# Separate key and value loads, a key store in rows of its own, and chunk-wise merging for mixer C in a two-layer hybrid encoder

## The chip, the core and the metric

One core of a Trainium2 chip runs the whole kernel. The metric is the device time of one execution in microseconds (us). The core has a matrix engine (TensorE, PE in the profile), a vector engine (VectorE, DVE), a scalar engine (ScalarE, ACT), GpSimd (POOL) and a sync engine (SyncE, SP), which here issues every DMA. Each engine works through its own list of instructions in order and waits on semaphores that the others raise. Sixteen DMA engines move the data between the chip's memory (HBM) and the on-chip memory (SBUF); matrix results land in eight banks of PSUM.

## What is computed

Two layers over two sequences of 256 and 512 tokens, width 2048. In each layer one projection gives queries, keys, values and gates for three attention mixers, whose outputs are gated, joined and projected back:

```
h = rms_norm(x, ln_g[l])
qa, ka, va, ga, qb, kb, vb, gb, qc, kc, vc, gc = split(h @ w_in[l])
ya = window_sink_attention(...)      # A: +-128 tokens, learned sink, relative bias
yb = global_axial_attention(...)     # B: dense, rotary positions
yc = dilated_mixture_attention(...)  # C: (window, dilation) = (128,1), (512,4), (2048,16)
mix = concat[ya * silu(ga), yb * silu(gb), yc * silu(gc)]
x = x + mix @ w_out[l]
```

In mixer C each of the three groups g gives an output and the logarithm of its softmax denominator, and the outputs are summed with softmax weights over these logarithms (the merge). There are 12, 12 and 8 query heads of 64 columns for A, B and C, and a quarter as many key and value heads.

## The kernel before, in words

The 768 tokens are six tiles of 128. A layer runs in three parts: the input projection (nine slabs of 512 columns, each 16 chunks deep), the attention with the gate projection woven in, and the output projection (four slabs). Every product is made of three matmuls on halves called hi and lo; weights arrive as `w_raw` and are split by ACT (`w_hi`) and DVE (`w_lo`).

At the end of the projection of a slab each head block is normalised, transposed and split, and SP stores it with four DMAs a tile into the DRAM tensor `heads_t` (tile, partition, block, 128 tokens), queries and keys alike; values go to `v_rows`. The values of the last slab go out in `store_values(l, NS_IN - 1, t)`, six DMAs.

The attention is a list of 216 steps a layer, in four sections. Section Q: four units of six steps, the dilated groups of mixer C, four heads a step (the "quads"). Section A: three units, 72 steps. Section C: the undilated group, two units, 48 steps. Section B: three units, 72 steps. In sections A, B and C an item is one tile for a pair of heads and takes two steps. A unit has one key head and one value head. All engines run the same loop over turns i: PE does `scores(i)`, some pieces of the gate projection (2.4 a turn in A, B and C, 0.6 in Q), then `p_turn(i - 3)` and the product with the values, `pv(i - 4)` or `pair_pv(i - 5)`. DVE does `find_minima(i)`, ACT `exp_step(i)`. `scores(i)` may not run until `find_minima(i - 2)` has freed its bank. The first `find_minima` of a layer waits until all value stores have landed (`v_stored`), since its output lies over the buffer that they read.

Loads. `load_unit(l, u)` brings keys and values of a unit into one of two slots: four DMAs for the keys (64 partitions each, six runs of 512 B in each partition) and one for the values, all counted on `kv_loaded`; it waits until the product with the values of the unit two before is done, and SP reaches it two items before the new unit begins. `load_item(l, it)` brings the queries of an item, four slots, and waits for the scores of the item four before. `load_bias` brings a unit's bias rows, four DMAs for a quad unit. All of them, the weights and the stores lie in SP's one list, in the order written in the loop over `it`. Before the loop the order is `load_bias(0)`, `load_unit(0)`, four `load_item`, six `store_values`, `load_unit(1)`, `load_bias(1)`.

The merge. Quads leave their outputs and statistics in DRAM (`part_rows`). In section C each item loads them back (`part_in`, three slots), DVE works out weights in ten short instructions (`merge_minima`, `merge_weights`) with ACT's exponential in between, POOL scales and adds the parts (`merge`), and `finish_item` on DVE adds the item's own output, which lies in `o_bank[0]`. The next item's product writes that same bank, so `pv` waits for it:

```
                if st["r"] != 1 and it >= 1:
                    old = ITEMS[it - 1]
                    if old["kind"] == "Q":
                        pe.wait_ge(part_taken, l * N_QUADS + old["quad_no"] + 1)
                    elif old["kind"] == "C":
                        pe.wait_ge(mixed, l * N_PAIRS + old["pair_no"] + 1)
```

PE then transposes the finished item (`mix_turn`) into bank 5 and ACT copies it out (`mix_copy`).

Of the kernel before, what the change touches and what calls it, by code (L numbers as in the profile page):

```python
# [35 lines left out]
P = 128  # L36
# [58 lines left out]
def index_units():  # L95

    blocks = vs = 0
    at = {}
    for u in itertools.chain(*SLAB_UNITS):
        if UNITS[u][0] == "v":  # L100
            at[u] = vs
            vs += 1
        else:
            at[u] = blocks
            blocks += 1
    return at, blocks, vs


PLACE, BLOCKS, VHEADS = index_units()
# [54 lines left out]
SLAB_BLOCKS = [sum(r[3] for r in HEAD_RUNS[s]) for s in range(NS_IN)]  # L164
MAX_BLOCKS = max(SLAB_BLOCKS)

# [96 lines left out]
N_TURNED = N_PAIRS - N_MERGES  # L263
SUNK = np.cumsum([x["kind"] == "A" for x in STEPS]).tolist()
# [20 lines left out]
PART_IN_SLOTS = 3  # L285
STAT_SLOTS = 8
# [5 lines left out]
MIN_LAG = 1  # L292
MERGE_LAG = 1
WEIGHT_LAG = 2
# [3 lines left out]
X_LAG = 7  # L298
NORM_LAG = 1
PAIR_LAG = 5  # L300
FOLD_LAG = 6

# [90 lines left out]

def piece_schedule():
# [48 lines left out]
PRODUCT_TURN = [max(SILU_TURN[n], CHUNK_LAST[n] + X_LAG) + 1 for n in range(GATE_TILES)]  # L443
# [18 lines left out]
UNITS_AT = at_items((u, UNIT_LAST[u - KV_SLOTS] + V_LAG + 1) for u in range(KV_SLOTS, len(ATT_UNITS)))  # L462
# [5 lines left out]
def build(nc, x_prompt, x_sample, ln_g, w_in, q_norm_a, k_norm_a, sink_a, q_norm_b, k_norm_b,  # L468
          q_norm_c, k_norm_c, rel_bias, w_out, selector, rope, identity, y_prompt, y_sample):
    with ExitStack() as ctx:  # L470
# [7 lines left out]
        heads_t = dram("heads_t", [TT, P, BLOCKS * P])  # L478
        v_rows = dram("v_rows", [TOKENS, VHEADS * DH])
# [47 lines left out]
        mix = sb("mix", [P, 2, P])  # L527
        part_sum = sb("part_sum", [P, 2, 2, P])
        merge_min = sb("merge_min", [P, PART_IN_SLOTS, 2])
        merge_w = sb("merge_w", [P, PART_IN_SLOTS, 3, 2])  # L530
        merge_d = sb("merge_d", [P, PART_IN_SLOTS, 3, 2])
# [25 lines left out]
        part_in = sb("part_in", [P, PART_IN_SLOTS, 2, PART])  # L557
# [6 lines left out]
        v_split = sb("v_split", [P, TT, 2 * DH], F32R)  # L564
        prob = sb("prob", [P, P_SLOTS, P_COLS])
# [5 lines left out]
        quad_t = sb("quad_t", [P, Q_SLOTS, 4, P], F32R)  # L571
        top[0] = pt_at
# [26 lines left out]
        mix_bank = bank[5]  # L599
# [55 lines left out]
        kv_loaded = [sem(f"kv_loaded{i}") for i in range(KV_SLOTS)]  # L655
        bias_loaded = [sem(f"bias_loaded{i}") for i in range(2)]
        part_loaded = [sem(f"part_loaded{i}") for i in range(PART_IN_SLOTS)]
# [14 lines left out]
        merge_parts = sem("merge_parts")  # L672
        recips = sem("recips")
# [35 lines left out]
        def mixed_chunk(item):  # L709

            return CHUNK_ORDER.index(item["unit"]["chunk"] + item["hp"])

# [88 lines left out]

        def turned_parts(l, s, t):
# [15 lines left out]
        def turned_views(eng, l, i, parts):  # L818
# [5 lines left out]
            eng.wait_ge(pv_done, l * N_STEPS + free)  # L824
            src = pt_bank[(l * N_STEPS + i) % PT_BANKS][:, 0:st["tiles"] * P].rearrange("p (j n) -> p j n", n=P)
            return src, parts[:, a % 2, 0:st["tiles"], st["r"], :]

        def heads_in_dram(eng, l):

            for i in range(2):  # L830
                eng.wait_ge(heads_stored[i], 16 * 4 * ((heads_before(l + 1) + 1 - i) // 2))
# [5 lines left out]
        def _(sp):  # L837
# [26 lines left out]
            def stores(l, slot):  # L864
                for step, s, t in POST.get(slot, ()):
                    if step == "sums" and V_RUNS[s]:
                        store_values(l, s, t)
                    if step == "store" and HEAD_RUNS[s]:
                        i = HEAD_AT[l, s, t]
                        sp.wait_ge(turned_lo, i + 1)  # L870
                        b0, nb = PLACE[SLAB_UNITS[s][HEAD_RUNS[s][0][2]]], SLAB_BLOCKS[s]
                        for part in range(2):
                            dst = heads_t[t, part * DH:(part + 1) * DH, b0 * P:(b0 + nb) * P].rearrange("p (b e c) -> p b e c", e=2, c=P)
                            for e in range(2):
                                sp.dma_start(dst[:, :, e, :], turned[e * DH:(e + 1) * DH, i % 2, part, 0:nb // 2, :].bitcast(F32))\
                                    .then_inc(heads_stored[i % 2], 16)

            def load_unit(l, u):
# [8 lines left out]

                for part in range(2):
                    src = heads_t[:, part * DH:(part + 1) * DH, unit["k"] * P:(unit["k"] + 1) * P].rearrange("t p n -> p t n")
                    for to in range(2):  # L890
                        sp.dma_start(k_t[to * DH:(to + 1) * DH, slot, :, part, :].bitcast(F32), src)\
                            .then_inc(kv_loaded[slot], 16)
                if unit["kind"] == "Q":
                    sp.wait_ge(v_stored, 16 * (l * V_STORES + V_BEFORE_LAST))
                sp.dma_start(v_t[:, slot, :, :],
                             v_rows[:, unit["v"] * DH:(unit["v"] + 1) * DH].rearrange("(t p) n -> p t n", p=P))\
                    .then_inc(kv_loaded[slot], 16)
# [20 lines left out]
            def load_item(l, it):  # L918
# [11 lines left out]
                if item["kind"] == "C":  # L930
                    m = l * N_MERGES + item["merge_no"]
                    if m % N_MERGES == 0:
                        for i in range(PART_SLOTS):
                            sp.wait_ge(part_stored[i], 16 * (l + 1) * (N_QUADS // PART_SLOTS))
                    if m >= PART_IN_SLOTS:

                        sp.wait_ge(merge_parts, 2 * (m - PART_IN_SLOTS + 1))
                    sp.dma_start(part_in[:, m % PART_IN_SLOTS, :, :],
                                 part_rows[t * P:(t + 1) * P, :, unit["j"], hp, :]).then_inc(part_loaded[m % PART_IN_SLOTS], 16)
# [53 lines left out]
            for l in range(DEPTH):  # L993
# [28 lines left out]
                load_unit(l, 0)  # L1022
                for it in range(Q_SLOTS):
                    load_item(l, it)
                for t in range(TT):
                    store_values(l, NS_IN - 1, t)
                load_unit(l, 1)
                load_bias(l, 1)
                for it in range(Q_SLOTS, N_ITEMS + 1):
                    if it < N_ITEMS:  # L1030
                        load_item(l, it)
                    for u in UNITS_AT.get(it, ()):
                        if ATT_UNITS[u]["kind"] != "Q":
                            sp.wait_ge(v_stored, 16 * V_STORES * (l + 1))
                        load_unit(l, u)
                    for b in BIASES_AT.get(it, ()):
                        load_bias(l, b)
                    for i in PARTS_AT.get(it, ()):
# [33 lines left out]
        def _(pe):  # L1072
# [45 lines left out]
            def project_chunk(l, c):  # L1118
# [8 lines left out]
                for t in range(TT):  # L1127
                    if k == 0:
# [10 lines left out]
                        elif s == NS_IN and t == 4:  # L1139
                            pe.wait_ge(mixed, (l + 1) * N_PAIRS)  # L1140
# [34 lines left out]
            def scores(l, i):  # L1175
# [3 lines left out]
                if st["r"] != 1:  # L1179
                    pe.wait_ge(q_loaded[it % Q_SLOTS], 16 * (it // Q_SLOTS + 1))  # L1180
                    if st["t"] == 0 and st["hp"] != 1:
                        kv, times = kv_place(l, st["u"])
                        pe.wait_ge(kv_loaded[kv], 16 * 5 * times)
# [30 lines left out]
            def pv(l, i):  # L1214
# [4 lines left out]
                if st["r"] != 1 and it >= 1:  # L1219

                    old = ITEMS[it - 1]
                    if old["kind"] == "Q":
                        pe.wait_ge(part_taken, l * N_QUADS + old["quad_no"] + 1)
                    elif old["kind"] == "C":
                        pe.wait_ge(mixed, l * N_PAIRS + old["pair_no"] + 1)
                    else:
                        pe.wait_ge(mixed, l * N_PAIRS + old["pair_no"])
                values = v_t[:, kv_place(l, st["u"])[0], :, :]
# [802 lines left out]
```

## Time and profile before

| | |
|---|---|
| median of 3 runs | 3000.72 us (2998.91 to 3005.28) |
| the profiled execution | 2995.85 us, its span 2994.1 us |
| PE busy | 2907.6 us (97%) |
| DVE, ACT, POOL busy | 46%, 38%, 31% |
| mean granted TensorE clock | 0.983 |
| DMA, one queue, 340 MB | 39.5% of sixteen engines |

The profile gives for each engine its instructions, grouped by the line of the kernel; the idle time of the engine just before them and what ended it; the clock that the chip granted TensorE in a stretch, as a share of its full speed; and the issue and landing of each DMA. A wait that is put down to "issue" is one for which the profile shows no releaser. Matmuls are pipelined, so that a busy PE isn't a PE at its peak.

### The profile page before, as it was taken

Reading aid. Unit: us, or ns where it says so; the run is one execution under the profiler, and the core shown is the slowest. Engines: PE = TensorE matmul, PEld = TensorE weight load, DVE = VectorE, ACT = ScalarE, POOL = GpSimd, SP = SyncE. Lnnn points to the kernel's source line nnn. Section 1 sums busy time; section 2 is a strip of 40 time slices with the busy share of each in tenths; the row PEclk is TensorE's granted clock in tenths of the full one; section 3 lists DMA queues with packets and bytes.
Section 4 is the critical chain, followed back from the end, with each engine's and each line's share of the span. In section 5 each row is a group of like instructions: output and inputs, shape, how many; then the busy total and the mean of one; then the engine's idle time right before and its main releaser. Section 6 shows DMA issues by size and latency. Waiting matters only on the chain. (4 is left out here: it accounts for less than half of the span.)

```text
span 2994.1 us, 44065 instructions
## 1 busy us (share of the span) xinstructions
PE 2907.6 (97%) x15201; PEld 2580.0 (86%) x15201; DVE 1376.2 (46%) x3869; ACT 1143.6 (38%) x2865; POOL 942.8 (31%) x942
## 2 busy tenths in 40 slices
PE   8999999998998999999999999999989989999999
PEld 6888899988998899888888888998889988998887
DVE  3334433324777777522323344333247777775221
ACT  4322232225664466421322322222346644664110
POOL 0333323310664477300002333323007634772000
PEclk9999999998999999999999999999879999999999
DMA  4333334357443432433223433334664434324332
GB/s 163 84 111 103 108 105 113 108 153 187 116 118 90 127 105 75 148 122 106 99 85 90 110 111 104 99 99 111 174 166 116 121 90 130 102 71 155 110 101 92
DMA packets 409305, 342.80 MB, mean 114 GB/s; under 512 B 53527, under 2 KB 340407, under 8 KB 409084
## 3 DMA queue, kind: packets, MB, share of 16 engines
q1 hardware_dynamic: 409084, 339.98, 39.5%
q8 instruction: 123, 2.02, 0.3%
q14 instruction: 98, 0.80, 0.1%
HBM read 256.03 MB, written 83.86 MB: 114 GB/s over the span
## 5 line engine op out<-in xcount | busy, mean ns | idle before, releaser
L1144 PE MATMUL bank<-w_hi,act_hi 128*128 128x512 f32 x2496 | 1000.5, 401 | 4.3 <-DVE w_lo L1561 4.3
L1145 PE MATMUL bank<-w_lo,act_hi 128*128 128x512 f32 x2496 | 988.8, 396 | 0.0
L1146 PE MATMUL bank<-w_hi,act_lo 128*128 128x512 f32 x2496 | 988.7, 396 | 0.0
L1561 DVE TENSOR_TENSOR w_lo<-w_raw,w_hi 128x512 fp32r<-128x512 f32 x544 | 388.5, 716 | 640.7 <-ACT w_hi L1323 638.8
L1323 ACT CAST w_hi<-w_raw 128x512 fp32r<-128x512 f32 x544 | 335.8, 618 | 778.7 <-PE bank L1146 775.7
L1144 PEld LDWEIGHTS bank<-w_hi,act_hi 128*128 128x128 f32 x2496 | 517.8, 207 | 95.2 <-DVE w_lo L1561 5.2
L1146 PEld LDWEIGHTS bank<-w_hi,act_lo 128*128 128x128 f32 x2496 | 517.7, 207 | 94.7
L1145 PEld LDWEIGHTS bank<-w_lo,act_hi 128*128 128x128 f32 x2496 | 518.1, 208 | 88.9
L1924 POOL TENSOR_SCALAR prob<-prob,denom 128x256 f32<-128x256 f32 (+2 forms) x288 | 343.4, 1198 | 323.6 <-DVE denom L1694 323.4
L1167 PE MATMUL bank<-act_hi,w_hi 128*128 128x384 f32 x1024 | 351.2, 343 | 0.0
L1169 PE MATMUL bank<-act_hi,w_lo 128*128 128x384 f32 x1024 | 348.3, 340 | 0.0
L1168 PE MATMUL bank<-act_lo,w_hi 128*128 128x384 f32 x1024 | 347.8, 340 | 0.0
L1915 POOL TENSOR_TENSOR y<-y,gains 128x256 f32<-128x256 f32 (+1 forms) x144 | 153.0, 1076 | 317.5 <-DVE y L1594 317.5
L1627 DVE TENSOR_TENSOR turned<-bank,turned 128x512 fp32r<-128x512 f32 (+1 forms) x96 | 63.2, 658 | 340.4 <-ACT turned L1386 340.4
L1210 PE MATMUL bank<-ident,prob 128*128 128x128 f32 x1232 | 213.9, 281 | 5.3 <-POOL prob L1924 5.3
L1685 DVE TENSOR_TENSOR pt_lo<-bank,pt_hi 128x256 fp32r<-128x256 f32 (+2 forms) x288 | 153.5, 533 | 125.6 <-ACT pt_hi L1418 122.6
L1418 ACT CAST pt_hi<-bank 128x256 fp32r<-128x256 f32 (+2 forms) x288 | 132.9, 461 | 186.6 <-PE bank L1210 176.6
L1168 PEld LDWEIGHTS bank<-act_lo,w_hi 128*128 128x128 f32 x1024 | 195.9, 191 | 4.2
L1167 PEld LDWEIGHTS bank<-act_hi,w_hi 128*128 128x128 f32 x1024 | 195.5, 191 | 4.2
L1386 ACT CAST turned<-bank 128x512 fp32r<-128x512 f32 (+1 forms) x96 | 53.8, 560 | 375.9 <-PE bank L1115 375.9
L1169 PEld LDWEIGHTS bank<-act_hi,w_lo 128*128 128x128 f32 x1024 | 195.7, 191 | 0.0
L1210 PEld LDWEIGHTS bank<-ident,prob 128*128 128x128 f32 x1232 | 161.2, 145 | 16.9 <-POOL prob L1924 6.9
(97 smaller groups left out, 3579.9 us busy)
## 6 DMA issues: line engine op xcount, KB each, us to landing
w_raw<-w_in SPq DMA_DIRECT2D x144, 512.0 KB, 4.1
heads_t<-turned SPq DMA_DIRECT2D x336, 128.0 KB, 2.4
w_raw<-w_out SPq DMA_DIRECT2D x64, 512.0 KB, 4.1
q_t<-heads_t SPq DMA_DIRECT2D x192, 128.0 KB, 2.1
k_t<-heads_t SPq DMA_DIRECT2D x96, 192.0 KB, 3.6
w_raw<-w_in SPq DMA_DIRECT2D x32, 448.0 KB, 3.5
quad_t<-heads_t SPq DMA_DIRECT2D x48, 256.0 KB, 3.9
mix_rows<-mixed_t SPq DMA_DIRECT2D x32, 384.0 KB, 2.6
```

Of the source, the lines that this page charges most:

```text
L1144: pe.matmul(acc[t][:], hi, w_hi[:, n % W_RING, :], start=(k == 0), stop=False)
L1145: pe.matmul(acc[t][:], hi, w_lo[:, n % W_RING, :], start=False, stop=False)
L1146: last = pe.matmul(acc[t][:], lo, w_hi[:, n % W_RING, :], start=False, stop=(k == KC - 1))
L1167: pe.matmul(out, hi, act_hi[:, k, tokens], start=(k == 0), stop=False)
L1168: pe.matmul(out, hi, act_lo[:, k, tokens], start=False, stop=False)
L1169: last = pe.matmul(out, lo, act_hi[:, k, tokens], start=False, stop=(k == KC - 1))
L1210: last = pe.transpose(pt_bank[n % PT_BANKS][:, j * P:(j + 1) * P], prob[:, n % P_SLOTS, j * P:(j + 1) * P], ident[:])
L1323: nc.scalar.copy(w_hi[:, n % W_RING, :], w_raw[:, load % W_RAW, j, :]).then_inc(w_hi_done, 1)
L1561: nc.vector.tensor_tensor(w_lo[:, n % W_RING, :], w_raw[:, load % W_RAW, j, :], w_hi[:, n % W_RING, :].bitcast(F32), ALU.subtract).then_in ...
L1685: nc.vector.tensor_tensor(lo, src, hi.bitcast(F32), ALU.subtract).then_inc(pt_dve, 1)
L1915: ins = nc.gpsimd.tensor_tensor(v, v, g, ALU.mult)
L1924: nc.gpsimd.tensor_scalar(v, v, denom[:, pair % STAT_SLOTS, st["r"]:st["r"] + 1], None, ALU.mult)\
```

## The change

Keys get a DRAM tensor of their own, `keys_t` (key head, partition, tile, hi or lo, 128 tokens), in which one head's 6 KB for a partition lie in one run. A slab that holds queries and keys is stored with eight DMAs a tile instead of four. `load_unit` becomes `load_keys` and `load_values`. `load_keys` is one DMA of 768 KB into all 128 partitions; its source names the 64 rows twice. It waits for the last scores of the unit two before, and stands four steps earlier. The values keep their wait and stand one step later. Before the loop the second unit's keys, bias and values now stand ahead of the six value stores. In section C the items write two banks in turn; ACT copies each item's output to SBUF (`keep`), and the merge is made once for six items (a chunk): three loads, the weights, POOL's scaling in two halves and its addition, DVE's scaling and addition in two halves, and six transposes in two groups. The statistics of a pair have 12 slots instead of 8 and are freed earlier.

```diff
@@ heads and stores
+        keys_t = dram("keys_t", [KHEADS, DH, TT, 2, P])
...
+                        for part, e in itertools.product(range(2), range(2)):
+                            turned_from = turned[e * DH:(e + 1) * DH, i % 2, part, :, :].bitcast(F32)
+                            if nq:
...
+                            if nq < nb:
+                                k0 = PLACE[SLAB_UNITS[s][first + nq]]
+                                dst = keys_t[k0:k0 + nb - nq, :, t, part, :].rearrange("(b e) p c -> p b e c", e=2)[:, :, e, :]
+                                sp.dma_start(dst, turned_from[:, nq // 2:nb // 2, :]).then_inc(heads_stored[i % 2], 16)
@@ loads
+            def load_keys(l, u):
...
+                if u >= KV_SLOTS:
+                    sp.wait_ge(scored, l * N_STEPS + UNIT_LAST[u - KV_SLOTS] + 1)
+                elif l > 0:
+                    sp.wait_ge(scored, l * N_STEPS)
+                src = bass.AP(keys_t.tensor, unit["k"] * DH * TT * 2 * P, [[0, 2], [TT * 2 * P, DH], [1, TT * 2 * P]])
+                sp.dma_start(k_t[:, slot, :, :, :].bitcast(F32).rearrange("p t s n -> p (t s n)"), src).then_inc(k_loaded[slot], 16)
...
-                for part in range(2):
-                    src = heads_t[:, part * DH:(part + 1) * DH, unit["k"] * P:(unit["k"] + 1) * P].rearrange("t p n -> p t n")
-                    for to in range(2):
-                        sp.dma_start(k_t[to * DH:(to + 1) * DH, slot, :, part, :].bitcast(F32), src)\
-                            .then_inc(kv_loaded[slot], 16)
...
-UNITS_AT = at_items((u, UNIT_LAST[u - KV_SLOTS] + V_LAG + 1) for u in range(KV_SLOTS, len(ATT_UNITS)))
+KEYS_AT = at_items((u, UNIT_LAST[u - KV_SLOTS] + 1) for u in range(KV_SLOTS, len(ATT_UNITS)))
+VALUES_IN_AT = at_items((u, UNIT_LAST[u - KV_SLOTS] + PAIR_LAG + 1) for u in range(KV_SLOTS, len(ATT_UNITS)))
+MERGE_IN_AT = at_items((mc, end - 2 * TT + 1 + PAIR_LAG + 1 if mc == 0 else MERGE_END[mc - 1] + OWN_TURN + 2) for mc, end in enumerate(MERGE_END))
...
                 load_bias(l, 0)
-                load_unit(l, 0)
+                load_keys(l, 0)
                 for it in range(Q_SLOTS):
                     load_item(l, it)
+                load_values(l, 0)
+                load_keys(l, 1)
+                load_bias(l, 1)
+                load_values(l, 1)
                 for t in range(TT):
                     store_values(l, NS_IN - 1, t)
-                load_unit(l, 1)
-                load_bias(l, 1)
@@ section C
+                if st["kind"] == "C":
+                    o = user_bank(("C", it))
+                    if st["r"] == 0:
+                        user_bank_free(pe, l, ("C", it))
...
+            def keep(l, it):
...
+                nc.scalar.copy(o_keep[m % KEEP_SLOTS][:, item["t"], :], user_bank(("C", it))[:, 0:2 * DH]).then_inc(kept, 1)
...
+                if ATT_UNITS[u]["kind"] == "B" and ATT_UNITS[u - 1]["kind"] == "C":
+                    act.wait_ge(merge_parts, 3 * (l + 1) * MERGES)
...
+            def merge_own(l, mc, h):
...
+                nc.vector.tensor_tensor(v, v, w, ALU.mult).then_inc(merge_scaled, 1)
+                dve.wait_ge(merge_scaled, 2 * m + h + 1)
+                dve.wait_ge(merge_parts, 3 * m + 3)
+                nc.vector.tensor_tensor(own, own, part_heads[0][:, tiles, :], ALU.add).then_inc(merged, 1)
```

## Rows read from the trace of the kernel before

**Rows 1.** Waits of PE: line waited for, us in total, times, longest us.
```profile
PE bank L1234 <- DVE mix L1776: 23.7, 20, 3.0
PE bank L1192 <- issue: 13.6, 4, 4.2
...
PE bank L1192 <- DMA quad_t<-heads_t: 4.7, 2, 2.4
...
PE bank L1234 <- DVE mixed_t L1714: 3.8, 2, 1.9
PE bank L1234 <- DVE part_out L1722: 2.8, 2, 1.7
```

**Rows 2.** Windows by section: us, busy by engine, clock, DMA share, GB/s.
```profile
667.10:749.10 82.00, 67.12 (x474) 65.45 (x474) 39.86 (x229) 46.17 (x206) 2.02 (x2) 0.85 0.73 185
...
907.50:1040.50 133.00, 118.73 (x792) 114.53 (x791) 97.04 (x425) 57.20 (x189) 53.16 (x87) 0.96 0.41 109
1040.50:1214.00 173.50, 171.77 (x1132) 165.44 (x1131) 124.83 (x326) 110.23 (x285) 127.72 (x103) 1.00 0.29 86
2148.00:2237.60 89.60, 79.62 (x475) 77.91 (x474) 40.03 (x228) 46.13 (x206) 1.99 (x2) 0.71 0.67 170
...
2395.20:2528.10 132.90, 117.61 (x792) 113.22 (x791) 95.95 (x425) 57.33 (x189) 53.39 (x87) 0.97 0.41 110
```

**Rows 3.** Timeline of PE in section Q of layer 1: start, us, instruction, idle before.
```profile
2211.61 0.30 PE L1192 MATMUL bank<-k_t,quad_t 128*128 128x128 f32 x1 [3.14 <-issue]
```

**Rows 4.** Windows in section Q: full clock and half clock.
```profile
2198.00:2210.00 12.00, 10.46 (x90) 10.25 (x89) 7.47 (x40) 7.91 (x35) 0.00 (x0) 0.99 0.74 208
2163.00:2173.00 10.00, 10.00 (x48) 9.83 (x47) 4.15 (x21) 4.59 (x21) 0.00 (x0) 0.50 0.57 105
```

**Rows 5.** DMA issues: count, KB each, median us to landing.
```profile
k_t<-heads_t SPq DMA_DIRECT2D x96, 192.0 KB, 3.6
...
x_cols<-x_sample SPq DMA_DIRECT2D x8, 1024.0 KB, 8.2
```

**Rows 6.** Windows at the kernel's start, columns as in rows 2.
```profile
26.00:27.00 1.00, 1.00 (x7) 0.78 (x6) 0.00 (x0) 0.00 (x0) 0.00 (x0) 1.00 0.17 55
...
31.00:32.00 1.00, 1.00 (x7) 0.80 (x6) 0.00 (x0) 0.00 (x0) 0.00 (x0) 1.00 0.26 90
22.00:25.00 3.00, 3.00 (x11) 2.39 (x10) 1.82 (x4) 0.88 (x2) 0.00 (x0) 1.00 1.05 408
```

**Rows 7.** Timeline of SP at the kernel's start.
```profile
22.43 12.55 SPq L855 DMA_DIRECT2D w_raw<-w_in  x3
```

**Rows 8.** Timeline of SP before and in section Q of layer 0.
```profile
638.84 2.03 SPq L916 DMA_DIRECT2D bias<-bias_rows  x4
640.91 3.46 SPq L891 DMA_DIRECT2D k_t<-heads_t  x4
...
645.91 2.92 SPq L928 DMA_DIRECT2D quad_t<-heads_t  x4
655.18 3.82 SPq L861 DMA_DIRECT2D v_rows<-raw  x6
659.04 2.62 SPq L891 DMA_DIRECT2D k_t<-heads_t  x4
...
662.35 2.08 SPq L916 DMA_DIRECT2D bias<-bias_rows  x4
667.12 0.33 SPq L928 DMA_DIRECT2D quad_t<-heads_t  x1
```

**Rows 9.** Instructions by line: out<-in, count, busy us, mean ns, idle before.
```profile
L1944 POOL TENSOR_TENSOR mixed_t<-mixed_t,gate_t 128x768 f32<-128x768 f32 x32 | 60.6, 1894 | 0.2
...
L1776 DVE SCALAR_TENSOR_TENSOR mix<-bank,merge_w,part_sum 128x64 f32<-128x64 f32 x96 | 22.7, 278 | 0.0
...
L1738 DVE TENSOR_TENSOR merge_min<-merge_min,minus_max 128x2 f32<-128x2 f32 x48 | 17.8, 371 | 1.7
...
L1753 DVE TENSOR_TENSOR merge_d<-merge_w,denom 128x2 f32<-128x2 f32 x48 | 7.3, 153 | 0.0
```

More of the change, by code:

```diff
@@ L164 @@
 SLAB_BLOCKS = [sum(r[3] for r in HEAD_RUNS[s]) for s in range(NS_IN)]
+SLAB_QUERIES = [sum(r[3] for r in HEAD_RUNS[s] if r[0] == "q") for s in range(NS_IN)]
+assert all(n % 2 == 0 for n in SLAB_QUERIES)
+STORES = [4 * ((q > 0) + (n > q)) for q, n in zip(SLAB_QUERIES, SLAB_BLOCKS)]
 MAX_BLOCKS = max(SLAB_BLOCKS)
@@ L263 @@
 N_TURNED = N_PAIRS - N_MERGES
+PAIRS = [x for x in ITEMS if x["kind"] != "Q"]
+MERGES = N_MERGES // TT
+MERGE_END = [x["step"] for x in ITEMS if x["kind"] == "C" and x["t"] == TT - 1]
+MIX_GROUPS = ((0, 4), (4, TT))
 SUNK = np.cumsum([x["kind"] == "A" for x in STEPS]).tolist()
@@ L297 @@
 MIX_LAG = 5
-X_LAG = 7
 NORM_LAG = 1
@@ L301 @@
 FOLD_LAG = 6
+X_LAG = 7
+KEEP_LAG = 5
+MIN_TURN = 1
+EXP_TURN = 2
+WEIGHT_TURN = 3
+PARTS_TURN = 3
+OWN_TURN = 7
+MIX_TURN = 9
+assert N_PAIRS % STAT_SLOTS == 0 and STAT_SLOTS % TT == 0 and (N_PAIRS - N_MERGES) // 2 % TT == 0
 def features_first(st):
@@ L391, with merge_turns, bank_users @@
 N_LOOP = N_STEPS + TAIL
+def merge_turns(i, since, n=1):
+    return [(mc, i - end - since) for mc, end in enumerate(MERGE_END) if 0 <= i - end - since < n]
+def bank_users():
+    users = []
+    for i in range(N_LOOP):
+        for lag, kinds in ((PAIR_LAG, "AB"), (V_LAG, "C")):
+            if 0 <= i - lag < N_STEPS and STEPS[i - lag]["last"] and STEPS[i - lag]["kind"] in kinds:
+                users.append((STEPS[i - lag]["kind"], STEPS[i - lag]["item"]))
+        users += [("mix", (mc, g)) for mc, g in merge_turns(i, MIX_TURN, len(MIX_GROUPS))]
+    return users
+USERS = bank_users()
+USER_AT = {x: p for p, x in enumerate(USERS)}
 def piece_schedule():
@@ L1259, in pair_pv, with mix_turn @@
                 last.then_inc(pv_done, 2)
-            def mix_turn(l, it):
-                m = l * N_MERGES + ITEMS[it]["merge_no"]
-                pe.wait_ge(mixed, l * N_PAIRS + ITEMS[it]["pair_no"] + 1)
-                if m >= 1:
-                    pe.wait_ge(mix_copied, m)
-                pe.transpose(mix_bank[:, 0:P], mix[:, m % 2, :], ident[:]).then_inc(mix_turned, 1)
+            def mix_turn(l, mc, g):
+                m = l * MERGES + mc
+                first, end = MIX_GROUPS[g]
+                pe.wait_ge(merged, 2 * m + 2)
+                user_bank_free(pe, l, ("mix", (mc, g)))
+                out = user_bank(("mix", (mc, g)))
+                for t in range(first, end):
+                    last = pe.transpose(out[:, (t - first) * P:(t - first + 1) * P], o_keep[m % KEEP_SLOTS][:, t, :], ident[:])
+                last.then_inc(mix_turned, 1)
             for l in range(DEPTH):
@@ L1518, in _ @@
                         back_hi_part(l, n)
-                    if ends_merge(i - X_LAG):
-                        mix_copy(l, STEPS[i - X_LAG]["item"])
+                    for mc, g in merge_turns(i, MIX_TURN, len(MIX_GROUPS)):
+                        mix_copy(l, mc, g)
                 for n in range(BACK_SLOTS, BACK_LEAD):
```

345 lines of the change are left out of this document (185 added, 160 removed).

## The prediction

> **What bounds the kernel now.** I read the waits of PE first: its idle time says what the change can give back. PE is busy 97% of the span, and the largest wait is that of `pv` (L1234) for `mix`, 23.7 us in 20 times: section C's single output bank. Next come the first scores of a quad unit (L1192) behind "issue", 13.6 us in 4 [rows 1]. The windows by section then show where PE isn't busy: 14.9 of 82.0 us in Q of layer 0, 10.0 of 89.6 in layer 1, 14.3 and 15.3 in C, 1.7 in B [rows 2]. A gap looks like the one at 2211.6, 3.1 us [rows 3]; the key loads of that unit were issued 7 us before it, so it is a wait for keys, although the profile names no releaser.
>
> The clock column adds a second cost. The granted clock was 0.85 and 0.71 in Q, 0.96 and 0.97 in C [rows 2]: parts of these sections ran at 1.2 instead of 2.4 GHz, after gaps. Half clock costs nearly its half: at 0.50 PE made 48 matmuls in 10 us, at 0.99 it made 90 in 12 [rows 4]. Time at half clock is twice the missing share: 2 x 0.15 x 82.0 = 24.6 us in Q0, cost 12.3; 52 us in Q1, cost 26.0; in C 5.3 and 4.0. Taking idle time and this cost off gives a dense length of 54.8 and 53.6 us for Q, 113.4 and 113.6 for C. The pairs agree, so the dense length is real: 2.3 us a turn in Q, 2.4 in C. At most 27, 36, 20 and 19 us can be won, 102 in all.
>
> **The key load, the term that decides.** Before, a unit's keys are four loads of 192 KB, 3.6 us each to landing, all waited for together with the values [rows 5]. After, they are one load of 786 kB, issued six turns ahead instead of two. That lead is ample if all sixteen engines share it: between 3.6 us for 192 KB and 8.2 for 1024 KB, 768 KB take some 7 us [rows 5]. But the source counts the copies outermost: 2, then 64 rows. No transfer of before has so small an outermost count, so the trace doesn't show the price directly. The other end is that each copy is one engine's work. One engine moves 408/(16 x 1.05) = 24.3 GB/s in a full stretch, 20.2 at 26 us [rows 6]; half of 786 kB takes 16.2 us, at most 19.5, and some 1.3 until it has landed. I take 16.2. From 26 to 32 us only three to four engines' worth of work ran (share 0.17 to 0.26) [rows 6], while SP needed 12.55 us to hand over three weight loads [rows 7]. So work stays on the engine it was laid on, idle engines don't take it over, and what stands behind it waits.
>
> The Trainium skill's page "DMA: Bandwidth & Descriptors", section "Rules for kernel authors", says that an outermost dimension of size c below 16, for example a leading zero-stride broadcast, keeps a transfer on at most c engines. No row here shows such a case; by that rule it is the 16.2 us, without it the 7.
>
> Consequence 1, the start of Q. SP's order before is bias, keys, four quad items by 648.8, value stores at 655.2 to 659.0, and only then the second unit's keys (659.0) and bias (662.4) [rows 8]. The first `find_minima` needs the value stores. After, on the two engines: the bias is through near 646, first keys 662, four items (each 256 KB, 0.7 us of every engine) 665, values 666, second keys 682, bias 685, values 686, six value stores of 0.7 us 690, landed 691. The stores landed near 661 before and the first scores of Q were done at 667.1 (the next item's load, which waits for them, goes out then) [rows 8]. DVE waits there with all its list behind it, PE after `scores(1)`, ACT behind both: the turns start 23 us later, in each layer alike.
>
> Consequence 2, three more key loads in Q (units 2, 3 and 4). Each is issued after `scores(6k)`; behind it on the same two engines stand the bias (2.5 us) and the item for turn 6k + 5 (0.7 us and 1.3 to land). 16.2 + 2.5 + 0.7 + 1.3 = 20.7 us against five dense turns, 11.5. A unit then lasts 20.7 + 2.3 = 23 us instead of 13.8; half clock hides in it. Q becomes 23 for the start, 10 for the first six (short) turns, 5 for half clock after the long idle time, 3 x 23 = 69: 107 us. Against 82.0 and 89.6 that is +25 and +17, **+42 us**.
>
> Consequence 3, seven more key loads a layer in A, C and B. Queries are loaded three and a half items ahead. 16.2 plus bias, item and landing, 20 to 21 us, meets nine turns: 20 us in A (2.2 a turn), 21 in C and B. Three in A miss by about 1 us, the others fit: **+6** for two layers. Weight loads have five chunks of lead, some 37 us, and hide.
>
> **Section C.** Removed per item: `finish_item`, two of 278 ns, and ten short merge instructions, between 153 and 371 ns, about 2.1 us in all [rows 9]; 64 of DVE's 97 us in C. Added per chunk: 14 of these at up to 0.4 us and four of 384 columns at about 0.6, some 6 us for six items. ACT gets 24 copies of 128 columns (`keep`) and loses 24 equal ones (`mix_copy`). POOL gets four of about 1.0 us and one of 1.9 (768 columns) [rows 9] for three small ones an item. PE's work is the same. `pv` now waits for the `keep` of two items before, one turn old or more, so the 23.7 us go, with the 3.8 at the step from A to C [rows 1]. Late next is DVE at a chunk's turns 1 and 3: chains of 5 and 10 dependent instructions, 1.5 to 2.5 us in a turn of 2.4 that also holds about 1.1 us of its other work; PE may lose 0.5 to 1 us a chunk, 3 a layer. C saves 19.6 - 3 and 19.3 - 3: **-33 us**. The parts of a chunk are issued three turns ahead of their use and are 0.8 MB in runs of 512 B; near 5 us at share 0.41 against 7 fits. Bounds: -20 (late parts) to -39 (all).
>
> **Section B.** The last chunk's merge falls into B, where POOL is busy 127.7 of 173.5 us [rows 2]. 5.9 us of POOL in three turns, and ACT's copy of B's first values now waits for POOL's addition, with `exp` queued behind it and PE behind that. POOL falls 2 to 3 us behind, the transposes have about two turns of slack: 0 to 3 us a layer, **+3** for both.
>
> **Stores.** 24 tiles of slabs 1 and 3 need eight DMAs instead of four: an issue took about 0.65 us (2.62 for four) [rows 8], so 5.2 us of SP in two chunks of some 8.4 us, beside one weight load. The same bytes in the same 512 B runs. With some 1.3 us for the weight load SP still has 1.9 us to spare, and PE's list of waits has none in the projection that names a DMA: nothing. The single semaphores, the statistics slots and the later values (six turns of lead in Q) cost nothing.
>
> **Sum.** 42 + 6 - 33 + 3 = +18 us on the profiled 2995.85. That run lies 4.9 us below the median of the runs; the difference is applied to the median: 3019, and 3 for what the SP list itself holds back behind a full queue: 3022 us.
>
> **Rivals.**
> *All sixteen engines share the key load.* Then it lands in 7 us against 11 and more. The 13.6 us of key gaps go with their half clock. The second unit's bias lands before the first items are asked for, which shortens the quad gap (4.7 us in 2). What stays in Q is the `part_out` wait (2.8 in 2) [rows 1] and some half clock behind it: I allow 63 us for Q, -19 and -27. With C -33 and B +3: -76, **2925 us**. For it: the destination has 128 partitions, as in all loads that land fast. Against: work that stays where it was laid [rows 6, 7], and the pattern. It decides from a landing time under about 11 us. The Trainium skill's rule above speaks against it.
> *The key load holds SP too.* If a queue behind it admits little [rows 7], each of the seven later key loads keeps SP some 3 us too long and the queries land late: 7 x 2 x 3 = 42 more, **3064 us**. It decides from a block of about 12 us a load; the lead in A is spent already.
> *Section C doesn't gain.* Two banks, but DVE's chains or late parts put a gap at each chunk: -20 instead of -33 with the key load as forecast, 3035 us.
>
> **Chances.** Key load on two engines 0.84: of it 0.60 the forecast, 0.12 each for the two dearer rivals. All engines 0.16. Within the first case Q may come out 15 us lower (stalls and half clock overlap more than I count) or higher, so 2985 to 3065 holds nearly all of it. The range has to hold 8 in 10: 2965 to 3065, which leaves out most of the sixteen-engine case and a little above. A measurement of this kernel can't tell less than 0.2%, 6 us, from no change. Slower by more: 0.74; within: 0.07; faster: 0.19.
>
> **What would show it.** Right: the first `find_minima` of a layer comes more than 15 us after `scores(0)`; the wait of L1192 or of DVE's L1654 for quad items or value stores grows to over 60 us; Q lasts over 100 us; the key load lands 16 to 20 us after its issue, at a DMA share near 2/16. The waits of L1234 for DVE in C are under 4 us, and C lasts 115 to 118 us. Wrong: key loads that land within 8 us and a Q of some 60 us; or C windows still near 130. The forecast fails first if the two copies aren't two engines' work.

## The result: 3.1% slower

| | before | after |
|---|---|---|
| median of 4 runs each, same chip | 2999.81 us (2995.67 to 3005.28) | 3092.28 us (3091.66 to 3094.35) |
| ratio, with its 95% interval | | 1.031 (1.029 to 1.033) |
| span of the profiled execution | 2994.1 us | 3092.6 us |
| mean granted TensorE clock | 0.983 | 0.966 |

The forecast was 3022 us, 2965 to 3065: right in direction, 70 us too low, and outside its own range. All times below are medians of the runs at the usual granted clock; one run of experiment 10 (3507.51 us) and one of the kernel before beside it (4726.06 us) came at a mean granted clock of 0.75 and 0.56 and are left out.

The windows by section of the changed kernel, first layer in the upper four lines, second in the lower four, in the order Q, A, C, B. A section runs from its first `find_minima` to the next one's; the windows are rounded to whole us, the ledger below goes by the exact starts. Columns: busy time (instructions) of PE, weight loads, DVE, ACT, POOL; then granted clock, busy share of the DMA engines, GB/s.

```profile
688.00:792.00 104.00, 76.28 (x463) 74.08 (x464) 38.95 (x227) 45.91 (x206) 2.01 (x2) 0.70 0.46 137
792.00:965.00 173.00, 159.35 (x1030) 156.03 (x1029) 117.27 (x463) 100.08 (x283) 104.91 (x97) 0.96 0.39 105
965.00:1081.00 116.00, 112.58 (x791) 110.13 (x790) 66.67 (x206) 56.85 (x175) 39.64 (x36) 1.00 0.47 125
1081.00:1265.00 184.00, 175.66 (x1132) 168.29 (x1131) 126.13 (x330) 111.18 (x288) 130.00 (x102) 0.98 0.27 83
...
2220.00:2325.00 105.00, 77.32 (x466) 75.43 (x467) 39.60 (x230) 45.84 (x206) 2.00 (x2) 0.70 0.44 134
2325.00:2499.00 174.00, 159.95 (x1024) 156.64 (x1024) 116.60 (x460) 99.96 (x283) 104.54 (x97) 0.95 0.38 104
2500.00:2615.00 115.00, 112.32 (x787) 109.88 (x786) 66.38 (x205) 57.20 (x177) 39.06 (x35) 1.00 0.47 126
2615.00:2798.00 183.00, 175.15 (x1128) 167.73 (x1127) 125.56 (x329) 110.75 (x287) 129.80 (x102) 0.98 0.27 84
```

Beside the windows of before [rows 2], and with A's 158 us and B's 173.5 of before, this gives a ledger of both layers:

| | forecast | measured, layer 1 + layer 2 |
|---|---|---|
| start of Q (how much later it starts), plus Q itself | +42 | 20.8 + 22.3 and 20.5 + 15.1 = +79 |
| A (forecast: key loads of A, C and B) | +6 | 14.7 + 17.4 = +32 |
| C | -33 | -17.1 - 17.7 = -35 |
| B | +3 | 10.8 + 10.3 = +21 |
| sum | +18 | +97 |

The waits of PE name who is late. Columns: the waiting instruction, what ended the wait; us in total, times, longest.

```profile
PE bank L1336 <- DVE prob_t L893: 49.6, 8, 11.2
PE bank L1292 <- DVE part_out L1760: 39.2, 2, 20.2
PE bank L1296 <- DMA q_t<-heads_t: 16.0, 8, 4.0
PE bank L1296 <- DVE minus_max L1780: 12.4, 6, 5.0
PE bank L1363 <- DVE mixed_t L1819: 6.2, 4, 2.5
PE bank L1336 <- DVE part_out L1827: 5.7, 5, 1.7
PE bank L1351 <- issue: 5.5, 2, 2.7
```

C's wait for `mix` [rows 1] is gone. The first two lines, 89 us, are DVE being late, so the next view is who held DVE; these are its waits in Q (L1760 is `find_minima` of a quad):

```profile
DVE prob L1760 <- DMA part_rows<-part_out: 63.4, 6, 12.9
...
DVE prob L1760 <- DMA v_rows<-raw: 53.0, 2, 27.1
```

Two stores are what DVE waits for: the last value stores at the start (twice 20 us on PE), and, six times, the store of a quad's parts. `part_out` is a ring of eight, so `find_minima` of item 6k + 3 needs the store of item 6k - 5 to have landed. That store stands in SP's list behind a key load and its bias rows. From DMA issues and landings of one such stretch, 701.2 to 711.5 us (KB each, median us from issue to landing; the key load has no landing in this profile):

```profile
k_t<-keys_t SPq DMA_DIRECT2D x1, 768.0 KB
bias<-bias_rows SPq DMA_DIRECT2D x4, 128.0 KB, 8.3
quad_t<-heads_t SPq DMA_DIRECT2D x1, 256.0 KB, 2.5
part_rows<-part_out SPq DMA_DIRECT2D x1, 132.0 KB, 9.8
```

SP's timeline there (start, length, engine, line). The keys go out at 701.28, the four bias rows keep SP for 9.56 us, the part store follows at 711.43 and lands 9.8 us later, at 721.3:

```profile
701.28 0.50 SPq L972 DMA_DIRECT2D k_t<-keys_t  x1
701.82 9.56 SPq L1007 DMA_DIRECT2D bias<-bias_rows  x4
711.43 3.67 SPq L1061 DMA_DIRECT2D part_rows<-part_out  x1
```

DVE's timeline (in brackets the idle time before an instruction and what ended it): nothing after 712.9, on again at 721.43, just after that landing.

```profile
712.89 0.42 DVE L1827 COPY part_out<-bank 128x256 f32<-128x256 f32 x1 [2.53 <-PE bank L1336]
721.43 0.29 DVE L1760 CUSTOM_DVE_ANT_0 prob<-bank,bias 128x128 f32<-128x128 f32 x1 [8.12 <-DMA part_rows<-part_out]
```

How wide the key load is shows in the packets of a quiet part of another one, 803 to 811 us (share: busy share of sixteen DMA engines):

```profile
DMA packets 570, 0.87 MB, mean 109 GB/s; under 512 B 56, under 2 KB 504, under 8 KB 570
...
q1 hardware_dynamic: 570, 0.87, 31.4%
```

570 - 504 = 66 packets lie between 2 and 8 KB, the 6 KB rows of the keys. On two engines that is 33 each in 8 us, 0.24 us a row, and 64 rows each are 15.5 us a unit. On sixteen, 128 rows at that pace would be through in 2 us. The start and length of each single packet, which the trace keeps too, leave no doubt: of the load issued at 701.28 the 128 packets of 6,144 bytes run from 703.1 to 718.7 us, 0.234 us each in the median, and two of them are under way at a time for 15.0 of these 15.6 us. It is the same for all 24 key loads of the run, which take 15.4 to 17.9 us.

### The profile page after: what moved, and what is told of

Read it like the earlier page. It is cut to its first block and busy times, and to the rows that moved or that the text cites. A ratio compares the mean times of both kernels' runs of the same rounds, so it can differ in the third digit from the quotient of the medians.

```text
span 3092.6 us, 43340 instructions
## 1 busy us (share of the span) xinstructions
PE 2929.0 (95%) x15201; PEld 2601.3 (84%) x15201; DVE 1317.3 (43%) x3437; ACT 1143.8 (37%) x2841; POOL 920.5 (30%) x838
## 5 line engine op out<-in xcount | busy, mean ns | idle before, releaser
L1667 DVE TENSOR_TENSOR w_lo<-w_raw,w_hi 128x512 fp32r<-128x512 f32 x544 | 395.3, 729 | 661.8 <-ACT w_hi L1421 660.2
L1296 PE MATMUL bank<-k_t,q_t 128*128 128x256 f32 (+2 forms) x384 | 157.7, 411 | 32.0 <-DMA q_t<-heads_t 16.0
```

The source lines that it names most:

```text
L1296: pe.matmul(out, q, keys[:, st["a"]:st["b"], 0, :], start=True, stop=False)
L1667: nc.vector.tensor_tensor(w_lo[:, n % W_RING, :], w_raw[:, load % W_RAW, j, :], w_hi[:, n % W_RING, :].bitcast(F32), ALU.subtract).then_in ...
```

## Experiments

Each ran together with the kernel before on the same chip, on three chips in all, where the kernel before took 2998 to 3001 us; the intervals are 95% of the ratio to it. A difference of a few us between two experiments isn't told apart from none by the times alone. The theory T: the single key load runs on two engines, and everything behind it in SP's list waits.

**1. Sixteen engines for the keys.** Two transfers of 64 rows, with the leading repeat gone.

```diff
-src = bass.AP(keys_t.tensor, unit["k"] * DH * TT * 2 * P, [[0, 2], [TT * 2 * P, DH], [1, TT * 2 * P]])
-sp.dma_start(k_t[:, slot, ...], src).then_inc(k_loaded[slot], 16)
+src = keys_t[unit["k"]].rearrange("p t s n -> p (t s n)")
+for to in range(2):
+    sp.dma_start(k_t[to * DH:(to + 1) * DH, slot, ...], src).then_inc(k_loaded[slot], 16)
```

> The changed kernel, but each unit's keys come in two transfers of 64 rows of 6,144 bytes (one for each half of the partitions) instead of one whose leading dimension is the repeat of 2. The same rows, bytes, order and waits. Theory T (the single transfer runs on two engines, 64 rows each at 0.234 us = 15 us, and whatever is issued behind it waits): the 20 us at the start of each Q go (-41), Q falls from 104 to 75-85 us, A from 173-175 back to 158-160, C stays at 115-116, B falls by 2-5: 2,930 to 2,965 us. Rival R1 (the excess of A and B, 53 us in all, comes from the new order of work and the new waits, not from the key load): A stays at 170 or more and B at 184, 3,000 to 3,020 us. Rival R2 (it is the size of one transfer to 128 partitions that holds the queue, on however many engines): within 20 us of 3,092.

Measured: 2957.09 us (2948.19 to 2961.47), ratio 0.986 (0.983 to 0.989): 135 us off the changed kernel, and 1.4% faster than before. The profile's line for the keys and the first layer's windows (Q, A, C, B):

```profile
k_t<-keys_t SPq DMA_DIRECT2D x48, 384.0 KB, 5.7
```

```profile
667.00:739.00 72.00, 67.94 (x477) 66.23 (x477) 39.92 (x229) 45.69 (x205) 2.00 (x2) 0.83 0.75 204
739.00:896.00 157.00, 153.48 (x1031) 150.44 (x1030) 117.47 (x464) 100.43 (x285) 105.12 (x98) 1.00 0.44 117
896.00:1011.00 115.00, 112.50 (x791) 110.20 (x790) 66.73 (x206) 57.20 (x177) 39.43 (x35) 1.00 0.49 126
1011.00:1194.00 183.00, 175.43 (x1132) 168.09 (x1131) 126.13 (x329) 110.86 (x287) 130.35 (x102) 0.98 0.29 84
```

The 128 key packets of a unit are now through in 3.9 to 6.1 us, with some sixteen under way at the peak. The start, Q and A are repaired; R1 falls for A, R2 altogether. B stays at 183, against what T expected: its 10 us have another cause.

**2. The key load alone.** The kernel before with the key tensor and its single load, at the old place together with the values, and the old merge.

```diff
-for part in range(2):
-    src = heads_t[:, part * DH:(part + 1) * DH, ...]
-    for to in range(2):
-        sp.dma_start(k_t[to * DH:(to + 1) * DH, slot, :, part, :], src).then_inc(kv_loaded[slot], 16)
+src = bass.AP(keys_t.tensor, ..., [[0, 2], [TT * 2 * P, DH], [1, TT * 2 * P]])
+sp.dma_start(k_t[:, slot, ...], src).then_inc(kv_loaded[slot], 16)
```

> The kernel before with the keys' part of the change alone: keys in a DRAM tensor of their own, stored and loaded as the changed kernel does (one transfer a unit with the leading repeat of 2), but loaded where the old key loads stood, together with the values, and with the old merge of C. Theory T: Q grows to 100-108 us, A to 170-175, C (133 before) to 133-137, B to 175-177; the start of Q is later by 3 to 10 us, since the value stores stand ahead of unit 1's keys here: 3,060 to 3,100 us. Rival R1 (A and B lengthen through the new order of work): A stays at 158-162 and B at 173-175, 3,030 to 3,055 us.

Measured: 3184.04 us (3182.51 to 3190.74), ratio 1.063 (1.059 to 1.066), 84 us above the top of T's range. First layer (Q, A, C, B):

```profile
670.00:804.00 134.00, 71.00 (x464) 69.00 (x465) 40.15 (x229) 46.20 (x206) 1.98 (x2) 0.69 0.45 121
804.00:977.00 173.00, 157.21 (x1030) 153.84 (x1029) 116.89 (x462) 100.03 (x283) 105.14 (x98) 0.95 0.40 107
977.00:1137.00 160.00, 121.57 (x791) 117.10 (x790) 96.72 (x424) 57.39 (x189) 52.98 (x87) 0.90 0.34 91
1137.00:1311.00 174.00, 172.28 (x1135) 165.97 (x1135) 125.06 (x327) 110.28 (x285) 128.15 (x103) 1.00 0.28 86
```

Q is 134 us, C 160; each layer has seven pauses of 10.9 to 15.2 us on PE, in Q, up to the first units of A and in C, nearly the whole key load, because here it starts only two items ahead. A is about as expected, 173 and 176 us. B at 173.5 clears the key load of B's loss a second time.

**3. Long rows without anything else.** As 2, but with the two transfers of experiment 1.

> The kernel before with the keys in rows of their own, loaded in two transfers of 64 rows of 6,144 bytes (sixteen engines each) at the place of the old four, with the old merge of C. If e1's Q (72 and 78 us against 82 and 90 before) comes from the rows alone, Q is 70 to 80 us here, A, C and B as before (158, 133, 174): 2,970 to 2,982 us. If e1's shorter Q needs the earlier key load (keys apart from values), Q stays at 82 and 90 and the time within 5 us of before.

Measured: 2996.78 us (2989.6 to 3002.53), ratio 0.999 (0.997 to 1.000). Q is 83.3 and 83.6 us (before 82.0 and 89.6). So the rows alone are worth nothing that can be measured. The narrow transfer costs 187 us at this place (3184 - 2997) and 135 at the new one (3092 - 2957): at the new place, with the new merge, 52 of it are hidden. The step from here to experiment 1 is Q -11.6 and -5.4 (keys loaded earlier, apart from the values), A -0.8 and -2.9, C -19.0 and -18.3, B +9.8 and +10.0. It changes the place of the keys and the merge at once; that C's part is the merge's is read from the waits (those of `pv` for `mix` are there in experiment 3, 24.4 us in 19, and gone in 1), no run has the merge alone.

**4. Short rows at the new place.** The changed kernel with the keys in the four transfers of before.

```diff
+for part in range(2):
+    src = keys_t[unit["k"]][:, :, part, :]
+    for to in range(2):
+        sp.dma_start(k_t[to * DH:(to + 1) * DH, slot, :, part, :], src).then_inc(k_loaded[slot], 16)
```

> The changed kernel with each unit's keys in the four transfers of before (64 partitions, rows of 6 times 512 bytes, 192 KB each), taken from the new key tensor, at the new place ahead of the values. It parts the width of the transfer from the size of its rows. Theory T (what costs is two engines instead of sixteen, not the rows): within 25 us of e1, 2,955 to 2,982 us, A 157 to 160, C 115, B 183, Q 72 to 84. Rival (the long rows carry e1's gain over before): Q back at 82 and 90, 2,985 us or more.

Measured: 2958.68 us (2952.99 to 2964.52), the same as experiment 1. Four transfers in 512-byte runs do as well as two in 6 KB rows. The cost was the width of the transfer, neither the bytes nor the rows.

**5. Four engines.** Two transfers of 64 rows whose leading dimension counts 4.

```diff
+rows = TT * 2 * P
+src = bass.AP(keys_t.tensor, unit["k"] * DH * rows, [[rows, 4], [4 * rows, DH // 4], [1, rows]])
```

> The changed kernel with each unit's keys in two transfers of 64 rows whose leading dimension counts 4 (rows taken in the order 0, 4, 8, ..., so the features of the keys stand in another order than those of the queries: this part of the computation is changed). Same rows of 6,144 bytes, same number of transfers as e1. Theory T (the leading count is the number of engines, with no repeat of zero stride needed): 32 rows an engine at 0.234 us = 7.5 us a unit, between e1's 2 and the changed kernel's 15; Q 76 to 88 us, A 157 to 162: 2,962 to 2,995 us, with items behind a key load landing 9 to 12 us after their issue. Rival (only the zero-stride repeat narrows a transfer): as e1, 2,952 to 2,962 us.

Measured: 3014.49 us (3009.7 to 3017.68), ratio 1.005 (1.003 to 1.006): between the two, but 20 us above the expected range. (The keys' features stand in another order than the queries' here, so this kernel doesn't compute the layer; only its transfers are of use.) DVE's wait for the part stores goes with the width: 63.4 us on two engines, here 36.2, in experiment 1 it is 7.2:

```profile
DVE prob L1763 <- DMA part_rows<-part_out: 36.2, 6, 10.1
```

```profile
DVE prob L1762 <- DMA part_rows<-part_out: 7.2, 2, 4.0
```

The dimension's count sets the width, with or without a repeat: the rival falls. In the packets at most four rows are under way at a time but for short overlaps, for 8.9 of the 12.3 us of the load issued at 691.96. The expected 7.5 us were too few: a load took 9.7 to 14.7 us, since a row often took longer than 0.234 us (0.314 in the median of that load). With bias and store behind it the store landed 16.5 us after the keys' issue (20.0 on two engines), and Q was 95 and 91 us.

This is where the rule quoted in the prediction from the Trainium skill (page "DMA: Bandwidth & Descriptors", section "Rules for kernel authors") is borne out: leading 2 and leading 4 both narrowed the transfer. The same section advises one 128-partition transfer rather than two to the halves of the partitions; here two beat the one by 135 us, because the one had the repeat in front.

**6. Value stores first.** The order at the start of Q alone.

```diff
+for t in range(TT):
+    store_values(l, NS_IN - 1, t)
 load_keys(l, 1)
 load_bias(l, 1)
 load_values(l, 1)
-for t in range(TT):
-    store_values(l, NS_IN - 1, t)
```

> The changed kernel with the last value stores issued ahead of unit 1's keys, bias and values, nothing else. Theory T: the stores wait only for unit 0's key load, so the gap of 19-20 us on PE at the start of Q shrinks to 0-5 us; unit 1's bias then lands some 3 us later than now and holds unit 1 a little: 3,050 to 3,065 us. Rival (unit 1's keys and bias set the start anyway, the stores only happened to land with them): within 10 us of 3,092.

Measured: 3085.73 us (3084.16 to 3088.3), only 6.5 us off the changed kernel, and the two intervals of the ratio to before overlap: T misses, the rival's time holds. The turns do start 17.7 us earlier, but Q then lasts 119 and 118 us instead of 104 and 105. The pause has moved to the next queries, which stand behind unit 1's keys:

```profile
PE bank L1336 <- DVE prob_t L893: 49.4, 8, 10.9
PE bank L1292 <- DMA quad_t<-heads_t: 25.1, 2, 13.3
```

**7. Bias first.** In a turn that loads both, bias ahead of keys.

> The changed kernel with the bias loads of a turn issued ahead of the key load of the same turn. Theory T (in-order queue: the bias is late only because the key load is ahead of it): in A the waits of 5 us for the bias go, in Q the key load itself (17 us) and what is behind it stay the limit, so Q falls by 2-10 us each: 3,060 to 3,085 us. Rival (the bias rows, 128 overlapping rows of 768 to 1,536 bytes, are slow in themselves): no change, 3,088 to 3,096 us.

Measured: 3131.8 us (3130.57 to 3132.49), 39.5 us slower than the changed kernel. Both expectations fail. The bias rows do land in 4.9 us (median) now, so they aren't slow in themselves, but they weren't what the turns waited for. The part store stands behind both in either order. With four bias loads ahead, the keys are issued later (2.4 us behind the item load ahead of them, not 0.4), the store right behind them lands 21 us after its issue, and DVE's wait for it grows from 63.4 to 78.4 us. Q is 10 and 12 us longer than in the changed kernel, A 5 in each layer:

```profile
DVE prob L1760 <- DMA part_rows<-part_out: 78.4, 6, 17.4
```

**8. Part stores first.** In a turn that loads keys, the part store ahead of them.

> The changed kernel with the stores of Q's parts of a turn issued ahead of its key load. In the changed kernel the three long pauses of Q (steps 9, 15, 21) end with the landing of the store of items 1, 7 and 13, eight items back, which stood behind the key load. Theory T (everything behind the key load is late together): the pause then ends with the next thing in the queue, the item load, some 0.6 to 1 us later or earlier; Q falls by 0 to 6 us a layer: 3,080 to 3,092 us. Rival (the ring of eight part buffers is the one cover that fails): Q falls by 8 to 10 us for each of three units: 3,035 to 3,050 us.

Measured: 3085.58 us (3084.6 to 3087.0), Q 101.6 and 102.6 us (104.2 and 104.7 before the reordering), as T says. The store that was late isn't any more, but the next one and the next queries are:

```profile
PE bank L1292 <- DMA quad_t<-heads_t: 43.0, 6, 8.1
PE bank L1292 <- DVE part_out L1760: 38.8, 2, 19.5
```

Three reorderings bought 7, -40 and 7 us; widening the load bought 135. Whichever transfer was moved out from behind the keys, another with as little lead was there.

**9. B's loss.** On top of experiment 1, the transposes of a merged chunk one turn later.

```diff
-MIX_TURN = 9
+MIX_TURN = 10
```

> e1 (keys on sixteen engines) with the transposes of a merged chunk one turn later (10 instead of 9 turns after the chunk's last step), so that they no longer take the bank that the pair just before them has filled. Theory T (B's start: PE waits 2.5 and 0.6 us there for the drained sums of that pair, and a half-clock stretch of 3.4 us follows it): B falls from 183 to 178 to 180.5, 2,946 to 2,953 us. Rival (the wait moves to the second group or to the pair behind): B stays within 1 us, 2,955 to 2,960 us.

Measured: 2946.41 us (2944.61 to 2948.67), ratio 0.982 (0.980 to 0.984). B is 180.4 us in both layers, and C gains 1.9 too. In the changed kernel the second group of transposes takes the bank that B's pair has just filled, and waits for DVE to drain it, 2.5 us (the line of L1363 above); that wait is gone, and so is one of the two stretches of 3.4 us at a granted clock of 0.50 that B had in each layer.

**10. B's other wait.** Then, the merge ahead of the normalisation in POOL's turn. In the changed kernel PE stands 2.74 us before B's first product with the values. The timeline there reads as a chain: POOL's last merge addition ends at 1096.1, ACT's copy of B's values follows at once, then DVE's remainder, then PE:

```profile
1094.32 1.80 POOL L2059 TENSOR_TENSOR part_in<-part_in,part_in 128x768 f32<-128x768 f32 x1
...
1096.20 0.51 ACT L1529 CAST v_split<-v_t 128x384 fp32r<-128x384 f32 x1 [4.20 <-issue]
...
1096.75 0.56 DVE L1803 TENSOR_TENSOR v_split<-v_t,v_split 128x384 fp32r<-128x384 f32 x1 [4.97 <-ACT v_split L1529]
...
1097.41 0.36 PE L1351 MATMUL bank<-pt_hi,v_split 128*128 128x256 f32 x1 [2.74 <-issue]
```

> e8 with the merge's stages ahead of the normalisation in GpSimd's order of a turn. Theory T (the 2.7 us that PE waits at B's first value product come from the end of the last merge on GpSimd, 1,025.7 us in e8, which ScalarE's split of B's values follows at once, since they lie over the merged parts): that end comes 0.9 us earlier, B is shorter by 0.5 to 2 us, 2,941 to 2,946 us. Rival (B's first probabilities, normalised later, take over): no gain, 2,945 to 2,950 us.

Measured: 2941.47 us (2933.29 to 2946.81), ratio 0.980 (0.976 to 0.984): the time alone can't tell it from experiment 9. The trace can: B is 178.8 us in both layers, 1.6 less, the wait is 1.1 us instead of 2.7, and B's other half-clock stretch is gone too. But 1.3 us of waiting for POOL's normalisation are new, a part of what the rival said. B stays 5.3 us longer than before: PE stands about 4 us more, for DVE's sums (1.4), for POOL (1.3), for the values (1.1), and this isn't mended.

**11. Both, and part stores first.**

> e10 with the stores of Q's parts ahead of the key loads of their turn. With keys on sixteen engines a part store behind keys and bias lands 7 to 8 us after its issue, ahead of them 3 to 4 us. Theory T (the ring of eight part buffers still ends a pause of 2 us at one or two places of Q): Q falls from 73 to 70 to 72 us: 2,937 to 2,943 us. Rival (keys or items are then later by as much): within 2 us of e10.

Measured: 2933.6 us (2929.15 to 2936.64), ratio 0.978 (0.975 to 0.981): 158.7 us less than the changed kernel, 2.2% less than before. It is faster than both. Q is 71.6 and 69.2 us; Q of like kernels varies by some 5 us between executions (73.1 and 73.1 in 9, 74.3 and 78.3 in 10), so how much the store order gives isn't settled by one profile. B's second layer had a half-clock stretch again here and took 180 us.

## Why the prediction was right in direction and too low

**Key load on two engines: right.** Forecast 16.2 us on the engines, 15.4 to 17.9 in the packets; experiments 1, 4 and 5 show that it is the width. It was the term that decides, and the rival with all sixteen engines (2925) is what experiment 1 made true. It came to 2957, since Q was 72 and 78 us, not 63, and B holds the term below.

**Start of Q: the term was right.** 23 us forecast, 20.8 and 20.5 measured, on the chain described (DVE waits 53.0 us in 2 for the value stores; the prediction had asked for over 60). Experiment 6 adds what the prediction didn't say: the stores only stand for the whole queue, so that mending their order gives back some 3 us a layer.

**A unit of Q: this is the step that failed, and the dearest.** Forecast: 20.7 us from the key load's issue to the item of turn 6k + 5, then one turn of 2.3 us to the next key load, 23 us, with "half clock hides in it". The landing was good: the item behind the keys of 701.28 landed at 721.9, after 20.6 us. But DVE stood at the part store of the ring of eight, needed at turn 6k + 3 and landed at 721.27. The prediction followed the loads through the queue and left out the stores. After it three turns follow before the next keys can be issued (at 731.52), and they run at a low granted clock, 0.60 from 721 to 732 us, and take 10.2 us instead of 7.

```profile
721.00:732.00 11.00, 8.61 (x49) 8.54 (x50) 6.02 (x36) 5.70 (x26) 0.00 (x0) 0.60 0.54 157
```

20.0 + 10.2 = 30.2 us a unit, not 23 (30.2 to 30.9 in the four units between two key loads of Q); three units in two layers make 43 us, about the 37 missing in Q. Of the excess, 3 to 4 us a unit lie ahead of the scores of item 6k + 5, which begin 23.8 to 24.8 us after the key load's issue, and 4 us behind: from there to the next key load it is 6.1 to 6.5 us, not 2.3.

Which transfer ends the pause isn't the heart of it. In experiment 8 PE waits for the item, as forecast, and a unit still lasts 28.5 to 31.8 us: 21.5 to 23.8 to the item's scores, then 7.0 to 8.1 to the next key load. In the first unit of each layer PE doesn't stand in this last stretch at all. It is busy all through, at half clock:

```profile
725.00:733.07 8.07, 8.07 (x37) 7.97 (x37) 4.16 (x26) 3.19 (x16) 0.00 (x0) 0.50 0.58 170
```

So what failed is the price of what follows a pause. Half clock doesn't hide in the wait for the keys, since the turns between the end of a pause and the next key load are on the path. The sign "Q lasts over 100 us" came true by luck: the forecast's 107 us hold the 23 of the start, which leaves 84 from the first `find_minima` on, and that stretch measured 104 and 105.

**A: the size was off.** +6 forecast for seven key loads a layer, +32 measured in A, none to be seen in C. In each layer some 10 us are idle time (13.7 against 3.9 in the first) and 5 and 7 are busy time that grew, at a granted clock of 0.96 and 0.95. The forecast set one load of 20 to 21 us against nine turns and found them equal, as if nothing else stood in the queue. But SP is held too: behind the keys at 854.34 one query load keeps it for 11.91 us, so that the next is issued only at 871.3 us.

```profile
854.34 0.50 SPq L972 DMA_DIRECT2D k_t<-keys_t  x1
...
858.89 11.91 SPq L1019 DMA_DIRECT2D q_t<-heads_t  x1
```

This is the rival "the key load holds SP too" (+42): it was there, in A and in Q. And A's first `add_folded` waits for all part stores, twice 7 us on DVE, which stands in no list of the prediction; PE waits 5.0 us behind it. Experiment 1 shows that all of A's excess goes with the width of the load; how it divides between SP and these stores is open. The wait of DVE:

```profile
818.04 0.58 DVE L1819 TENSOR_TENSOR mixed_t<-bank,fold 64x128 f32<-64x128 f32 x2 [6.96 <-DMA part_rows<-part_out]
```

**C: right.** -33 forecast, -35 measured, 115 to 116 us as forecast, and the waits of `pv` there are 2.4 us for `keep` and 1.8 for `prob_t`, in both layers together. It stays whole at every width of the key load (115 us in 1, 4 and 5).

**B: the place was right, the size wrong.** The copy of B's first values behind POOL's addition was named and priced at 0 to 3 us. It costs 2.7 us a layer, and 3.4 us at half clock come with it. The transposes were said to have two turns of slack; in fact they wait for a bank that B's pair shares, 2.5 and 0.6 us, with a second such stretch. In sum PE is idle 6.6 us longer (8.3 against 1.7) and busy 4 us longer for the same matmuls, 10 to 11 a layer. The failing step here is the new list of bank users: it was followed through C, where the change puts it to use, not through the turns of B that it reaches into. Experiments 9 and 10 take back 4 to 5 of these us.

**Stores:** nothing, as said. With the wide load the first layer's Q starts at 667.2 us (experiment 1) against 667.1 before, after the same eight stores a tile as in the changed kernel.

The range failed because three errors (Q, A, B) had one sign. Its upper end was the time of one rival alone (3064); nothing in it allowed for that rival together with a unit of Q that was priced too low.

## What to carry to other kernels

Look at the outermost count of a transfer's source before its size: 2 in front of 64 rows made 768 KB a matter of 15 to 18 us and of everything queued behind it, and splitting it in two gave 135 us. When a slow transfer stands in one in-order list, go through all that stands behind it, stores and rings of buffers included, and ask for each at which turn it is needed; here reordering only handed the wait to the next. Price the turns that follow a pause at the half clock, and ask whether they lie on the path to the next pause; here they did, and 2.3 us became 6 to 8.

## What the runs showed of the hardware

- A transfer's width followed its leading count: with 2, 4 and 64 in front a unit's 128 key rows were under way two, up to four and some sixteen at a time, took 15.4 to 17.9, 9.7 to 14.7 and 3.9 to 6.1 us, and gave DVE waits of 63, 36 and 7 us for the store behind them.
- Behind a narrow transfer the issuing engine was held too: single issues took up to 13.8 us. Most take 0.3 to 0.6, and in experiment 1 none but weight loads took over 2.5.
- The profile shows no landing time for the transfers on two or four engines, while it does for those on sixteen. Their length was read from the packets.
- Pauses cost twice: B's two, 2.5 and 2.7 us, came with two stretches of 3.4 us at a granted clock of 0.50, one of which went with each pause that was mended (experiments 9 and 10), and Q's PE time in layer 1 rose from 67 to 76 us while its granted clock fell from 0.85 to 0.70 [rows 2].
